# Moving small triangular-inverse products and two projection jobs among the dense products of a two-layer DeltaNet and attention trunk

## The reference, cut to what matters

```python
u = _rms_norm(x, pre_mix_norm_w[l])
proj = u @ w_in[l]          # q,k,v, z, a,b, cq, ckv, k_rope, gate logits
qkv_a = silu(_causal_conv(qkv_a, conv_w[l]))
...
lower = jnp.where(strict, kk, 0.0) + jnp.eye(CHUNK)
sol = triangular_solve(lower, rhs, lower=True, unit_diagonal=True)
...                          # per chunk: v_new, o, state
o_a = _rms_norm(o_a, gdn_norm_w[l]) * silu(z_a)
y_a = o_a @ w_branch_a[l]
q_b = _rms_norm(cq, q_a_norm_w[l]) @ w_uq[l]
kv_b = _rms_norm(ckv, kv_a_norm_w[l]) @ w_ukv[l]
y_b = _chunk_causal_attention(q_b, k_b, v_b) @ w_branch_b[l]
h = gates[:, :, 0] * y_a + gates[:, :, 1] * y_b
x = x + _rms_norm(h @ w_out[l], post_mix_norm_w[l])
x = x + _rms_norm(square(relu(_rms_norm(x) @ w_ff1[l])) @ w_ff2[l])
```

## Time and profile before

| | |
|---|---|
| median of 3 runs | 1038.16 us (1035.57 to 1040.65) |
| the profiled execution's own time | 1044.89 us |
| its span, first to last instruction | 1043.1 us |
| PE busy | 1019.8 us (98%) |
| PE weight load busy | 990.7 us (95%) |
| DVE / ACT / POOL busy | 733.4 (70%) / 558.7 (54%) / 100.0 (10%) us |
| mean granted TensorE clock | 0.992 of full speed |
| HBM read | 161.25 MB, 156 GB/s |

### The profile page before, as it was taken

How to read it: one execution, slowest core, us unless ns; L and a number is a source line. 1 busy time by engine, 2 the same in 40 slices (tenths; PEclk the granted TensorE clock), 3 DMA queues, 4 the chain that set the end, 5 groups by cost and what they waited for, 6 DMA issues and landing times.

```text
span 1043.1 us, 24322 instructions
## 1 busy us (share of the span) xinstructions
PE 1019.8 (98%) x10626; PEld 990.7 (95%) x10626; DVE 733.4 (70%) x1024; ACT 558.7 (54%) x791; POOL 100.0 (10%) x76
## 2 busy tenths in 40 slices
PE   9998999999999999999999989999999999999996
PEld 8998999899999999999999989998999999999995
DVE  7887568697576788654598665677865777885543
ACT  7675475746445544434466634767554445544441
POOL 0010001310000222100000100015000003221000
PEclk9999999999999999999999989999999999999998
DMA  8543433434565466666535444334356646666661
GB/s 293 163 138 127 122 98 109 122 125 166 174 188 178 136 202 190 202 198 188 179 112 172 121 124 124 104 120 126 100 181 183 185 137 188 197 189 200 197 182 41
DMA packets 45609, 163.86 MB, mean 157 GB/s; under 512 B 5184, under 2 KB 5440, under 8 KB 45504
## 3 DMA queue, kind: packets, MB, share of 16 engines
q1 hardware_dynamic: 45360, 162.16, 50.4%
q10 hardware_dynamic: 144, 0.15, 0.0%
HBM read 161.25 MB, written 1.05 MB: 156 GB/s over the span
## 4 chain that ended last, share of the span: by engine, by line
PE 88%; DVE 7%; issue 2%; ACT 2%; DMA 0%; SPq 0%; DVEq 0%; ACTq 0%
PE dense L610 23%; PE dense L611 22%; PE dense L612 22%; DVE wlo L1455 2%; PE sides L922 1%; PE sides L1075 1%; PE sides L1049 1%; PE sides L1050 1%; PE sides L910 1%; PE dense L593 1%; PE dense L594 1%; PE sides L594 1%; PE sides L593 1%; PE dense L595 1%; PE sides L595 1%
## 5 line engine op out<-in xcount | busy, mean ns | idle before, releaser
L1455 DVE TENSOR_TENSOR wlo<-raw,whi 128x1024 fp32r<-128x1024 f32 (+1 forms) x303 | 392.6, 1303 | 196.9 <-ACT whi L1110 196.4
L1110 ACT ACTIVATE whi<-raw 128x1024 fp32r<-128x1024 f32 (+2 forms) x305 | 316.0, 1044 | 222.3 <-PE dense L612 201.6
L610 PE MATMUL dense<-uh,whi 128*128 128x256 f32 x768 | 224.8, 293 | 2.7 <-DVE ul L1484 1.3
L611 PE MATMUL dense<-ul,whi 128*128 128x256 f32 x768 | 215.3, 280 | 0.0
L612 PE MATMUL dense<-uh,wlo 128*128 128x256 f32 x768 | 215.1, 280 | 0.0
L610 PEld LDWEIGHTS dense<-uh,whi 128*128 128x128 f32 x768 | 146.6, 191 | 5.1 <-DVE ul L1484 1.4
L611 PEld LDWEIGHTS dense<-ul,whi 128*128 128x128 f32 x768 | 146.0, 190 | 1.3 <-issue 1.0
L612 PEld LDWEIGHTS dense<-uh,wlo 128*128 128x128 f32 x768 | 146.0, 190 | 0.0
L610 PE MATMUL dense<-fuh,whi 128*128 128x256 f32 x512 | 142.8, 279 | 0.4 <-DVE ful L1827 0.4
L611 PE MATMUL dense<-ful,whi 128*128 128x256 f32 x512 | 141.9, 277 | 0.0
L612 PE MATMUL dense<-fuh,wlo 128*128 128x256 f32 x512 | 141.9, 277 | 0.0
(11 more groups left out here) (320 smaller groups left out, 2095.5 us busy)
## 6 DMA issues: line engine op xcount, KB each, us to landing
raw<-weights SPq DMA_DIRECT2D x304, 512.0 KB, 3.9
xT<-x_t SPq DMA_DIRECT2D x4, 256.0 KB, 5.3
out_t<-xT SPq DMA_DIRECT2D x4, 256.0 KB, 2.3
cst<-consts SPq DMA_DIRECT2D x1, 512.0 KB, 8.1
prm_all<-params ACTq DMA_DIRECT2D x1, 150.0 KB, 3.8
pos_i<-pos SPq DMA_DIRECT2D x1, 128.0 KB, 7.8
cst<-consts SPq DMA_DIRECT2D x1, 6.0 KB, 7.6
```

The costliest lines, as they stand in the source:

```text
L610: mm(o_, h_[:, ws], ahi[:, k0 + k, :], start=is_first, stop=False, skip_group_check=True)
L611: mm(o_, h_[:, ws], alo[:, k0 + k, :], start=False, stop=False, skip_group_check=True)
L1110: return A(o_, i_, ACT.Copy)
L1455: TT(wlo[s][:, 0:w], raw[s][:, 0:w], f32(whi[s][:, 0:w]), ALU.subtract).then_inc(lo_ready, 1)
```

## The change

Before, the eight level steps stand 24 products apart, except 48 about the steps `lvP` 2 and `lvV` 2, where job `gate` 0 lies. After, they stand 48 (behind `lvP`) and 24 (behind `lvV`) apart. Job `gate` 0 goes behind the `q` jobs, and `kn` 0 to 3 between `t_ks`, `t_v1` and `qk`, so the stretch from `lvP` 0 to `pairP` holds 48 products more and the state steps that many less. `vt` jobs move ahead with them: `vt` 0 now stands ahead of `qk` 0 and `kr`. In the last loop the output norm's steps change places: `osq` i now comes behind `onrm` i-1, with one `uq` job to `onrm` i.

```diff
-                                  ("z", range(1, 4), 2), ("v", range(2), 2), ("gate", range(1), 2), ("v", range(2, 4), 2),
-                                  ("q", range(4), 2),
+                                  ("z", range(1, 4), 2), ("v", range(4), 2), ("q", range(4), 2), ("gate", range(1), 2),
...
-    between = [(kind, part, i) for kind in "vq" for i in range(4) for part in (half, job)]
-    behind = {n: [] for n in range(len(between) + 3)}
+    units = [(kind, part, i) for kind in "vq" for i in range(4) for part in (half, job)]
+    units += [("gate", half, 0), ("gate", job, 0), ("kn", job, 0), ("kn", job, 2)]
+    shares = [2, 1] * 4 + [1] * 8
+    ready = {n: [] for n in range(len(units))}
+    behind = {n: [] for n in range(len(shares))}
     for n in range(8):
-        behind[2 * n + 2].append(("conv", 4 + n))
-        behind[2 * n + 3].append(("silu", 4 + n))
+        ready[2 * n + 2].append(("conv", 4 + n))
+        ready[2 * n + 3].append(("silu", 4 + n))
...
-    for n, (kind, part, i) in enumerate(between):
-        if steps[n][0][0] in ("lvP", "lvV"):
-            LEVEL_STEP[JOBS[JOB["gate", 0]][2][1] if n == 4 else JOBS[JOB[kind, i]][2][n % 2]] = steps[n][0]
-        if n == 4:
-            half("gate", 0)
-        o.extend(steps[n])
-        if n == 4:
-            job("gate", 0)
-        part(kind, i)
+    at_unit = 0
+    for n, share in enumerate(shares):
+        for at_ in range(share):
+            kind, part, i = units[at_unit]
+            if at_ == 0:
+                o.extend(steps[n])
+                if n < 2 * len(SIZES):
+                    LEVEL_STEP[JOBS[JOB[kind, i]][2][int(part is job)]] = steps[n][0]
+            part(kind, i)
+            if kind == "kn":
+                job(kind, i + 1)
+            o.extend(ready[at_unit])
+            at_unit += 1
         o.extend(behind[n])
...
+    o.append(("q2", 0))
+    job("vt", 0)
     o += [("qk", 0), ("qk", 1), ("qd", 0), ("kr", 0)]
...
-    o.append(("t_o", 1))
     job("vt", 3)
-    o.append(("osq", 0))
     for n, i in enumerate((4, 5, 0, 1, 2, 3)):
         job("uq", i)
         if i >= 4:
             late.append(("qrope", i - 4))
-        if 1 <= n <= 4:
-            o.append(("onrm", n - 1))
-        if n < 3:
-            o.append(("osq", n + 1))
+        if n == 0:
+            o.append(("t_o", 1))
+        if n >= 2:
+            o.append(("onrm", n - 2))
+        if 1 <= n < 5:
+            o.append(("osq", n - 1))
```

More of the change, by code:

```diff
@@ L191, in schedule @@
     steps += [[(step, 0), (step, 1)] for step in ("t_v0", "t_st", "t_ks", "t_v1")]
-    for n, (kind, part, i) in enumerate(between):
-        if steps[n][0][0] in ("lvP", "lvV"):
-            LEVEL_STEP[JOBS[JOB["gate", 0]][2][1] if n == 4 else JOBS[JOB[kind, i]][2][n % 2]] = steps[n][0]
-        if n == 4:
-            half("gate", 0)
-        o.extend(steps[n])
-        if n == 4:
-            job("gate", 0)
-        part(kind, i)
+    at_unit = 0
[11 more added lines that the diff above has]
+            at_unit += 1
         o.extend(behind[n])
-    job("kn", 0)
-    o += behind[16] + [("q2", 0)]
-    job("kn", 1)
+    o.append(("q2", 0))
+    job("vt", 0)
     o += [("qk", 0), ("qk", 1), ("qd", 0), ("kr", 0)]
-    job("kn", 2)
-    o += behind[17]
-    job("kn", 3)
+    job("vt", 1)
     o += [("q2", 1), ("q2", 2), ("q2", 3), ("lnexp", 1), ("t_o", 0)]
-    job("vt", 0)
+    job("vt", 2)
     o += [("qk", 2), ("qk", 3), ("qd", 1)]
-    job("vt", 1)
-    job("vt", 2)
-    o.append(("t_o", 1))
     job("vt", 3)
-    o.append(("osq", 0))
     for n, i in enumerate((4, 5, 0, 1, 2, 3)):
```

## The result

| | before | after |
|---|---|---|
| median of 4 runs | 1039.41 us (1035.57 to 1045.07) | 1055.93 us (1054.95 to 1057.81) |
| the profiled execution's own time | 1044.89 us | 1054.95 us |
| its span | 1043.1 us | 1053.2 us |

The changed kernel is slower: ratio 1.0155, 95% interval 1.0122 to 1.0187, or 16.5 us. The forecast was 1047 us, with a range that ended at 1055. The direction was right; the size forecast, 8.8 us, was about half of what came.

What follows compares the result with a forecast made beforehand. TensorE, busy 98%, was taken as the bound. The norm's 8.8 us plus about 0 for the level steps took the profiled 1044.9 to 1053.7 us; with the median 6.7 us lower, 1047 us, range 1041 to 1055.

Steps and rivals of the forecast that it cites:

- What bounds the kernel, and that late instructions are behind the issue waits: Whole kernel: TensorE, busy 98%, bounds it; its "issue" waits in the level steps are instructions that come late.
- Output norm: Last loop: TensorE waits 1.4 to 1.5 us for GpSimd's addition at three sums a layer, 8.8 us in both layers.
- The mask's wait gone, `XTq` the new wait at `lvP` 2: Level steps: VectorE's 1.06 us mask wait goes; TensorE waits for VectorE's transpose ahead of `lvP` 2, 2.5 to 4 us, twice.
- The chain that I wrote: Level steps, `lvV` 0 to `lvP` 2 through ScalarE and VectorE: 21.1 us, against 17.0 us that TensorE alone needs.
- The sum for the profiled execution: Whole kernel: 8.8 us for the norm and about 0 for the level steps, from 1044.9 to 1053.7 us.
- the term of the level steps: `lvP` 0 to `pairP`: gains of 2.8, 1.1 and 0.2 us against 4 us of clock falls, about 0 us together.
- The clock's charge: Behind `lvP` 2: TensorE's idling brings the clock down again, 2 us in each layer, 4 us; bounds nothing and 3 a layer.
- Rival 2: Longer low clock behind `lvP` 2, `t_o` 1 waits, plain runs never had the profiled losses: 1053 us; chance 0.20.
- Rival 1: Level steps: no clock fall behind `lvP` 2, so their 4.1 us gain stands against 8.8: 1043 us; chance 0.16.
- Rival 4: Output norm: its waits don't arise, GpSimd or ScalarE being faster, and level steps come out even: 1038 us; chance 0.04.
- Rival 3: Level steps: late-instruction pauses and clock falls, up to 14 us, go and outrun the norm: 1033 us at best; chance 0.05.
- Moved jobs: `kn`, `gate` 0 and `vt` 0 in their new places: no time counted, up to 1 us a layer left to the range.

Runs made afterwards that it cites:

- Experiment 3: Kernel before with its eight warm-up products replaced by 52 small ones, moving later TensorE instructions 176 places along; median 1039.8 us, ratio 0.9993.
- norm_alone: Kernel before with only the last loop's new output norm order; median 1051.1 us, ratio 1.0099.
- levels_alone: Changed kernel with the output norm's old order, so only the new level-step spacing and moved jobs; median 1047.5 us, ratio 1.0060.
- wide_before: Kernel before with 12 products instead of 6 between the two parts of each level step; median 1038.7 us, ratio 0.9979.
- shift_before: Kernel before with 52 small warm-up products in place of eight, shifting later TensorE instructions by 176 places; median 1039.8 us, ratio 0.9993.

## Why the prediction came out too low

**What bounds the kernel, and that late instructions are behind the issue waits:** held. Experiment 3 ties the pauses to the count of instructions and to the landing of their packets. The Trainium skill (Runtime: NRT & Kernel Launch, Instruction fetch mechanics) says that the crossing of such a block is mostly hidden. For most of this kernel the traces agree: the long pauses put down to instructions all lie in the level steps. In the level steps they don't: up to 3.0 us at one crossing.

**Output norm:** the mechanism held in every member, six waits at L1026. The term was mis-sized a little: the trace has 5.0 us a layer (35.29 us in `norm_alone` against 30.29 before, `t_o` 0 to first scores), not 4.4. The first addition takes 1.69 us, not 1.32, which makes its turn 4.76 us; and the sum behind a wait takes 1.12 us, not 1.02. In plain runs it is 10.6 us by the medians and 10.1 by the mean spans: 8.8 in the rest and 1.2 in the clock, the last about as much as a clock on record to 0.001 can tell from nothing.

**The mask's wait gone, `XTq` the new wait at `lvP` 2:** both held, 2.0 us on average at `lvP` 2. The chain that I wrote, 21.1 us from `lvV` 0, came to 24.1. I had counted the wait as "4.1 us less whatever instruction wait there was on the way", as if a pause on TensorE could hide in the chain. It can't: a member of the chain is the evacuation of `v` 1, which TensorE makes late when it pauses or runs slowly itself (VectorE's idle 6.33 us). That, and not the table load, is the difference: the Trainium skill's 1.38 us of drain (ScalarE: Activation LUTs, What ACT_TABLE_LOAD costs) would have lengthened the chain too. But the rows speak against it: SiLU starts 1.29 us after the load began, and over the twelve traces the operation behind a table load starts as early as this in 96 of the 156 loads.

**The sum for the profiled execution:** 1053.7 us was forecast, 1054.95 measured. The stretch from `lvP` 0 to `pairP` was to be 28.3 + 24.75 + 2 = 55.05 us (0.4 more in the first layer), and is 56.94 and 54.95. The total is 1.3 us too low. That is partly luck: the norm took 1.2 us more in both layers than its term and these stretches 1.4 us more than written here, and more than 1 us came back elsewhere, which I didn't trace. Within the stretches, the way to `lvP` 2 took 31.8 and 31.2 us, not 28.3, the 3 us of the chain, and the 2 us charged for the clock covered most of it.

**The step that failed** is the term of the level steps, "2.8 + 1.1 + 0.2 - 4 = about 0 us", taken over from the profiled execution to the plain runs: there the level steps cost 7.0 us (`levels_alone`), 5.6 of them clock. The norm was 1.8 us over its term of 8.8, and the level steps 7.0 over nothing; 1.1 of this sum isn't seen in the 16.5 us of the whole change. What carried the error into the forecast is the sentence behind the sum: "The median of the runs is 6.7 us below the profiled one. The same difference would give 1038.2 + 8.8". Seen from there, the miss of 8.9 us is 1.3 of the sum, 1.0 by which the median after lies above its own profiled run, and the 6.7 us that I took off. A kernel has no constant difference between its profiled execution and its median. The profiled execution of before was one of its longer ones (6 of 74 plain runs were longer): mean granted clock 0.992, a clock loss of 8.3 us, where plain runs have 5.9 to 6.9 on average, and a rest 1.7 to 2.4 us above theirs. Its losses in the level steps, some of which my estimate of the gain gave back, are thus larger than those of the usual run. The new order's losses are not: in `levels_alone` the profiled run, at 0.992, was one of the lucky ones (its median is 0.989). Compared profile to profile, the level steps of `levels_alone` cost nothing; over all runs they cost 7.0 us.

**The clock's charge** of 2 us a layer for the new falls was too low: the profile of the changed kernel has 6.7 us, against the 4 charged. For the plain runs, take 3.3 us as the part of the clock loss that lies behind TensorE's last product, the mean of the twelve profiles (an estimate; plain runs have no trace). Then `levels_alone` has 8.2 us from its level steps, and `wide_before`, 4.1 in all, has 0.8. The kernel before has 2.6 to 3.6, where its profiled execution had 5.1: that much less was there to win back.

**Rivals.** Rival 2 had the mechanism that the forecast lacked: longer low clock, and plain runs without the losses that the profiled one shows. Its time, 1053, was the nearest, in part by luck: its third member, a wait at `t_o` 1 of 2 us, didn't come up. Rival 1 is refuted: the clock did fall behind `lvP` 2 in the first layer. It did not in the second (window 630 to 642 us at 1.0), after a wait that was even longer, 2.22 us. Rival 4 is refuted by the waits at L1026. Rival 3 is refuted by the level steps: they still had their pauses, 5.1 us of issue waits against 7.3, and lost time in plain runs.

**Moved jobs:** held at nothing. From `t_v1` to the first scores the kernel before takes 43.02 us with 48 products more, 37.56 without them; `levels_alone` takes 37.49.

**What stays open:** which of the level steps' pauses a given execution gets, and why. The same code between `lvP` 0 and `pairP` took 45.75 us in the second layer of `norm_alone` and 50.51 in the profile before. A pause ends 1.2 to 1.5 us after its packet has landed, but what sets the start of that packet relative to the stream no run here shows.

## What to carry to other kernels

A profile is one execution. Where the loss that a change is to win back is a pause or a clock fall, look first at the spread of the plain runs and at the clock that each of them reports: in this kernel that column alone held 5.6 of the 6.2 us by which the mean span rose with the new level steps, a rise that a comparison of two profiles gave as zero.

In a chain that goes around through several engines, put the work that the next turn needs ahead of the work that ends this turn: the square ahead of Ln and Exp gave back 4.4 us a layer in the trace by swapping two statements. A chain with a member that the waiting engine itself produces takes up that engine's pauses; don't credit them against the wait.

Spread small matmuls evenly. Six products more between the parts of a step, one digit in the code, were worth 2.6, 4.6 and 5.0 us in three orders of this kernel.

## What the runs showed of the hardware that I had not expected

- Useless work can pay: filling a wait of 2 us with useless products (8 a layer, 1.8 us) made the kernel 2.7 us faster by the medians, with the clock loss down from 11.5 to 6.6 us. How much of this is the filled wait, and how much the shift of the later instructions, isn't separated.
- A pause doesn't always bring the clock down. 2.22 us ahead of `lvP` 2 in the second layer and the norm's six waits of 1.2 to 1.7 us were followed by a granted clock of 1.0; 1.83 us ahead of `lvP` 2 in the first layer was followed by 1.2 GHz within 1.3 us.
- TensorE's instructions come in 16 KiB packets of 256 (21,548 instructions and 84 packets in the trace of before, 176 more and 85 in `shift_before`). Among the dense small matmuls of the level steps TensorE paused at some of these packets, for up to 3.0 us, always at the same counts, and went on 1.2 to 1.5 us after the packet had landed.
- The mean granted clock of an execution holds stretches that cost nothing: after TensorE's last product the clock fell in each of the twelve profiles, which counts as 2.5 to 4.0 us of clock loss in kernels whose whole figure is 4 to 13.
